# A streaming-encoder block on eight cores: pool branch over two blocks at once, group mixing folded into the output weights, conditioning by dot products

## The reference

```python
cc = silu(c)
mod = (cc @ w_ada + b_ada).reshape(b, 9, D)      # shift, scale, gate for three sub-layers
h = rms_norm(x, g_ffn1) * (1 + sc1) + sh1
x = x + 0.5 * gt1 * swiglu(h, w_ffn1_in, w_ffn1_out)
h = rms_norm(x, g_mix) * (1 + sc2) + sh2
z = h @ w_in                                      # q, k, v, u, gate A, gate B
ya = chunk_band_attention(q, k, v, ...) @ w_attn_out
mixed = trailing_mean(u, window of the group) - u
yb = (einsum(mixed, w_pool_group) * pool_scale) @ w_pool_out
x = x + gt2 * ((sigmoid(ga) * ya + sigmoid(gb) * yb) @ w_o)
h = rms_norm(x, g_ffn2) * (1 + sc3) + sh3
x = x + 0.5 * gt3 * swiglu(h, w_ffn2_in, w_ffn2_out)
```

## Time and profile before

| | us |
|---|---|
| median of 3 runs | 1546.69 (1546.11 to 1546.8) |
| the profiled execution, its own time | 1544.76 |
| its span on the slowest core (core 7) | 1543.2 |
| spans of the eight cores | 1537.7 to 1543.2 |
| TensorE busy | 1486.7 (96%) |
| VectorE busy | 815.5 (53%) |
| ScalarE busy | 451.3 (29%) |
| POOL busy | 119.4 (8%) |

### The profile page before, as it was taken

The page is one execution under the profiler, slowest core; times in us unless marked ns, Lnnn a source line. Parts: engine busy times, 40 slices in busy tenths (PEclk is TensorE's granted clock), DMA queues, the critical chain, the costliest instruction groups (busy, mean ns, idle before and its releaser), DMA issues.

```text
span 1543.2 us, 23259 instructions; the slowest of 8 cores (1537.7 to 1543.2 us)
## 1 busy us (share of the span) xinstructions
PE 1486.7 (96%) x8336; PEld 703.2 (46%) x8336; DVE 815.5 (53%) x1290; ACT 451.3 (29%) x630; POOL 119.4 (8%) x170
## 2 busy tenths in 40 slices
PE   2899999999999999999999999999999999999998
PEld 1344444444444444454564454444444444444443
DVE  2366344172272756678765568746453616162644
ACT  3470111101101036468855453523401010101010
POOL 1100100100001012200000000203000000000000
PEclk9999999999999999999999999999999999999999
DMA  9951433513515211430044363347132221211022
GB/s 204 243 102 28 76 69 55 99 25 69 96 28 102 48 41 38 123 60 15 1 93 86 56 130 63 69 82 116 28 55 53 44 42 16 47 28 28 1 110 109
DMA packets 24303, 107.13 MB, mean 69 GB/s; under 512 B 2816, under 2 KB 3072, under 8 KB 21760
## 3 DMA queue, kind: packets, MB, share of 16 engines
q0 software_dynamic: 21312, 75.67, 29.0%
q1 hardware_dynamic: 2880, 29.98, 5.6%
HBM read 168.71 MB, written 12.58 MB: 117 GB/s over the span
## 4 chain that ended last, share of the span: by engine, by line
PE 91%; DMA 3%; DVE 3%; issue 2%; ACT 1%; POOL 0%; DVEq 0%; ACTq 0%; POOLq 0%
PE ps L714 44%; PE ps L742 21%; PE ps L1081 7%; PE ps L887 4%; PE ps L1113 4%; PE ps L1094 3%; DMA arena<-w_ada 3%; PE ps L1027 2%; DVE arena L513 1%; PE ps L933 1%; PE ps L969 1%; PE ps L870 1%; DVE arena L519 1%; PE ps L563 1%; PE ps L609 1%
## 5 line engine op out<-in xcount | busy, mean ns | idle before, releaser
L714 PE MATMUL ps<-arena 128*128 128x512 bf16 x3152 | 694.4, 381 | 4.4 <-DVE arena L519 4.0
L507 ACT ACTIVATE arena<-ps 128x512 bf16<-128x512 f32 (+3 forms) x426 | 268.5, 652 | 946.3 <-PE ps L714 790.4
L714 PEld LDWEIGHTS ps<-arena 128*128 128x128 bf16 x3152 | 307.8, 98 | 376.3 <-issue 16.2
L519 DVE SCALAR_TENSOR_TENSOR arena<-ps,arena 128x512 f32<-128x512 f32 (+1 forms) x500 | 360.4, 748 | 73.6 <-ACT arena L507 22.6
L513 DVE TENSOR_TENSOR arena<-arena,ps 128x512 bf16<-128x512 bf16 x198 | 135.1, 687 | 486.8 <-PE ps L714 476.1
L742 PE MATMUL ps<-arena 128*128 128x512 bf16 x1584 | 345.0, 379 | 1.3 <-DVE arena L513 1.2
L742 PEld LDWEIGHTS ps<-arena 128*128 128x128 bf16 x1584 | 154.4, 98 | 188.3 <-issue 5.5
L513 DVE TENSOR_TENSOR arena<-arena 128x1024 f32<-128x1024 f32 (+8 forms) x228 | 173.6, 780 | 33.8 <-ACT arena L507 27.6
L1081 PE MATMUL ps<-arena 128*128 128x512 bf16 x512 | 116.3, 379 | 1.4 <-ACT arena L507 1.0
L507 ACT ACTIVATE arena<-arena 128x512 f32<-128x512 f32 (+2 forms) x86 | 89.3, 1053 | 35.2 <-DVE arena L519 20.8
L1081 PEld LDWEIGHTS ps<-arena 128*128 128x128 bf16 x512 | 49.1, 98 | 59.8 <-issue 2.4
(11 more groups left out here) (65 smaller groups left out, 516.6 us busy)
## 6 DMA issues: line engine op xcount, KB each, us to landing
arena<-w_ada POOLq DMA_DIRECT2D x36, 512.0 KB, 8.8
arena<-w_gate POOLq DMA_DIRECT2D x24, 512.0 KB, 8.5
arena<-w1i POOLq DMA_DIRECT2D x22, 512.0 KB, 6.5
arena<-w3i POOLq DMA_DIRECT2D x22, 512.0 KB, 5.3
arena<-x SPq DMA_DIRECT2D x5, 2048.0 KB, 15.5
outT<-arena SPq DMA_DIRECT2D x8, 1024.0 KB, 3.9
arena<-w1o POOLq DMA_DIRECT2D x10, 512.0 KB, 6.8
arena<-w_kqvu POOLq DMA_DIRECT2D x10, 512.0 KB, 7.6
```

Source lines behind the costliest of these rows:

```text
L507: return e.activation(out=o, in_=i, func=func, scale=scale)
L519: return e.scalar_tensor_tensor(out=out, in0=in0() if callable(in0) else in0, scalar=scalar, in1=in1() if callable(in1) else in1, op0=op0, ...
L714: ins = e.matmul(pst(t), lhsT=w[:, kt, :], rhs=hk(b, kt), start=(kt == 0), stop=(kt == 7))
```

## The change

- The pool branch treats both blocks of a pass as one row of 16 + 1024 columns. The history is copied once per group, the additions run over up to 1040 columns, the subtraction over 1024.
- Group mixing and pool scale go into the pool output weights: `fold()`, ahead of the third group of the first FFN, scales the (now transposed) group weights on VectorE, multiplies them with w_pool_out in 8 matmuls of 512 columns, evicts on ScalarE and stores the bf16 result in the first block's part of the output tensor, from which `gates` reads it through SP's queue. The mixing matmul, its scaling and POOL's load of the group weights go. The last store of that block waits for the reads.
- Columns 24 to 71 of the conditioning (groups 12 to 35) are computed on VectorE: w_ada's transpose comes in 48 fp32 tiles of 128x1024 through SP's queue into two buffers, and one `scalar_tensor_tensor` each multiplies it with the silu of c on every partition and sums along the row. They run behind three of every four units from the 23rd on.
- `norm_apply` gives six of eight tiles to ScalarE in the second and third sub-layer, three of eight in the first as before.
- The matmuls of `outp` also wait for the gate's row; the last block is stored in pieces of 4, 2, 1 and 1 tiles where it was 4 and 4.
- Some planned costs and all due times in `RAMPS` are other numbers.

```diff
-RAMPS = {"v0a": (6.86, 12.16), "k0a": (10.15, 11.87), "k0b": (10.76, 11.77), "v0b": (12.6, 12.7),
...
+RAMPS = {"v0a": (15.71, 38.08), "k0a": (10.87, 12.53), "k0b": (11.92, 12.65), "v0b": (18.64, 26.23),
...
+    def ada_dot(j, deps=()):
+        wt = ADS[j % 2]
+        S.op("sp", lambda e: e.dma_start(out=wt, in_=adat_d[j - 24]), writes=[wt], dma="d_ads%d" % (j % 2), nbytes=1 << 19,
+             deps=deps)
+        S.op("dve", lambda e: e.scalar_tensor_tensor(out=wt, in0=wt, scalar=1.0, in1=CCB, op0=ALU.mult, op1=ALU.mult,
+                                                     accum_out=MOD[:, j:j + 1]),
+             reads=[wt, CCB], writes=[wt, MOD[:, j:j + 1]], cost=1.22)
...
-                if kt in (1, 4, 7):
+                if kt in ((1, 4, 7) if sub == 0 else (0, 1, 3, 4, 6, 7)):
...
+    def fold():
+        pgf = view(wslot("f"), F32, (4, 128))
+        S.op("sp", lambda e: e.dma_start(out=pgf, in_=wpg_d.rearrange("p (g n) -> p g n", g=4)), writes=[pgf], dma="d_wpg",
+             nbytes=1 << 18)
+        for g in range(4):
+            ts(WPG[:, g, :], pgf[:, g, :], CST[:, 106 + g:107 + g], ALU.mult, [pgf, CST], [WPG], 0.2)
+        wps = [load("f", po_d[q])[0] for q in range(2)]
+        outs = [view(wslot("f"), BF16, (2048,)) for _ in range(2)]
+        for g in range(4):
+            for hf in range(2):
...
+                S.op("pe", lambda e, t=t, g=g, src=src: e.matmul(pst(t), lhsT=WPG[:, g, :], rhs=src, start=True, stop=True),
+                     reads=[WPG, wps[g // 2]], writes=[t], cost=mmc(1, 512))
...
+        for hf in range(2):
+            ov = outs[hf].bitcast(F32)
+            FOLD.append(S.op("sp", lambda e, ov=ov, hf=hf: e.dma_start(
+                out=outT[0].rearrange("p a b -> p (a b)")[:, 1024 * hf:1024 * (hf + 1)], in_=ov),
+                reads=[outs[hf]], dma="d_fold%d" % hf, nbytes=1 << 19))
...
-            if ada_next[0] < 36 and n > 20 and n % 3 == 0:
-                c = ada_next[0]
-                ada_load(c, [uops[max(0, n - 7)]])
-                t = Tile()
-                ada_mm(c, t, c)
-                ada_out(t, c, 1)
+            if ada_next[0] < 72 and n > 22 and n % 4 != 0:
+                j = ada_next[0]
...
+                ada_dot(j, [uops[max(0, n - 4)]])
...
-                            for n in range(0, 8, 4):
...
+                            for n, w in ((0, 4), (4, 2), (6, 1), (7, 1)) if b == blocks[-1] else ((0, 4), (4, 4)):
...
+                if first and g == 2:
+                    fold()
...
-                mx = MIXED[:, gq, mb * TB:(mb + 1) * TB]
-                stt(mx, src[:, 16:528], 1.0 / (2 << gq), ub[:, 16:528], ALU.mult, ALU.subtract, [src, ub], [mx], 0.75)
...
-                S.op("pe", lambda e, ty=ty, gq=gq, mx=mx: e.matmul(pst(ty), lhsT=WPG[:, gq, :], rhs=mx, start=True, stop=True),
-                     reads=[WPG, mx], writes=[ty], cost=mmc(1, 512))
-                ts(mx, lambda ty=ty: pst(ty), CST[:, 106 + gq:107 + gq], ALU.mult, [ty, CST], [mx], 0.7)
...
+                tt(dst[:, lo:1040], src[:, lo:1040], src[:, lo - sh:1040 - sh], ALU.add, [src], [dst], 1.28)
...
+            mx = MIXED[:, gq, :]
+            stt(mx, src[:, 16:1040], 1.0 / (2 << gq), ub[:, 16:1040], ALU.mult, ALU.subtract, [src, ub], [mx], 1.45)
...
-            wap = load("m", gate_d[3 * c + 2])[0]
...
+            S.op("pool", lambda e, c=c, wap=wap: e.dma_start(out=wap[:, 0:1024], in_=ao_d[c]), writes=[wap[:, 0:1024]],
+                 dma="d_w%d" % o_ap, nbytes=1 << 19)
+            wpf = view(o_ap + 2048, F32, (512,))
+            USES.append(S.op("sp", lambda e, c=c, wpf=wpf: e.dma_start(
+                out=wpf, in_=outT[0].rearrange("p a b -> p (a b)")[:, 512 * c:512 * (c + 1)]), writes=[wap[:, 1024:2048]],
+                dma="d_wf%d" % o_ap, nbytes=1 << 18, deps=[FOLD[c // 2]]))
```

More of the change, by code:

```diff
@@ L383, in build_nc @@
     cst_d = din("cst", [128, NCST])
-    ada_d = din("w_ada", [36, 128, 2048])
+    ada_d = din("w_ada", [12, 128, 2048])
+    adat_d = din("w_adat", [48, 128, 1024])
+    crow_d = din("crow", [128, 1024])
     w1i = din("w1i", [22, 128, 2048])
@@ L389, in build_nc @@
     kqvu_d = din("w_kqvu", [8, 128, 2048])
-    gate_d = din("w_gate", [12, 128, 2048])
+    gate_d = din("w_gate", [8, 128, 2048])
+    ao_d = din("w_ao", [4, 128, 1024])
+    po_d = din("w_po", [2, 128, 2048])
     wo_d = din("w_o", [4, 128, 2048])
@@ L585, in der @@
                  reads=[src], writes=[dst])
+    ADS = [view(o_expb + 4096 * i, F32, (1024,)) for i in range(2)]
+    CCB = view(o_kq, BF16, (1024,))
+    def ada_dot(j, deps=()):
[5 more added lines that the diff above has]
+             reads=[wt, CCB], writes=[wt, MOD[:, j:j + 1]], cost=1.22)
     rk_pos = [0]
@@ L744, in mm @@
                     return ins
-                S.op("pe", mm, reads=[w for w in wos] + [ACTB[:, jl, b, :] for jl in range(nk)], writes=[t],
+                S.op("pe", mm, reads=[w for w in wos] + [ACTB[:, jl, b, :] for jl in range(nk)] + [DER[:, 3 * sub + 2, :]], writes=[t],
                      cost=mmc(nk, 512))
@@ L832, in build_nc @@
     ffn(w1i, w1o, 0, [0, 1, 2, 3, 4], True)
-    S.op("pool", lambda e: e.dma_start(out=WPG, in_=wpg_d.rearrange("p (g n) -> p g n", g=4)), writes=[WPG], dma="d_wpg",
-         nbytes=1 << 18, deps=[S.ops[-1]])
     S.op("pool", lambda e: e.dma_start(out=IDENT, in_=ident_d), writes=[IDENT], dma="d_idn", nbytes=1 << 16,
@@ L1017, in u_stage @@
                 ts(UH[:, gq, :], lambda th=th: pst(th, 0, 16), CST[:, 110:111], ALU.mult, [th, CST], [UH[:, gq, :]], 0.17)
+            S.op("dve", lambda e, gq=gq: e.tensor_copy(out=ub[:, 0:16], in_=UH[:, gq, :]), reads=[UH[:, gq, :]],
+                 writes=[ub[:, 0:16]], cost=0.17)
             for mb in range(2):
@@ new lines, in u_stage @@
+            src = ub
+            for st in range(gq + 1):
+                sh = 1 << st
+                dst = TTS[st % 2]
+                lo = 2 * sh - 1
+                tt(dst[:, lo:1040], src[:, lo:1040], src[:, lo - sh:1040 - sh], ALU.add, [src], [dst], 1.28)
+                src = dst
+            mx = MIXED[:, gq, :]
+            stt(mx, src[:, 16:1040], 1.0 / (2 << gq), ub[:, 16:1040], ALU.mult, ALU.subtract, [src, ub], [mx], 1.45)
+            if pas == 0:
+                t16 = TTS[(gq + 1) % 2]
+                tt(t16[:, 0:16], src[:, 16:32], CST[:, 112 + 16 * gq:128 + 16 * gq], ALU.mult, [src, CST],
+                   [t16[:, 0:16]], 0.17)
+                tt(MIXED[:, gq, 0:16], t16[:, 0:16], ub[:, 16:32], ALU.subtract, [t16[:, 0:16], ub],
+                   [MIXED[:, gq, 0:16]], 0.17)
@@ L1238, in _prep @@
         gates.append(_cols(w_in, 3072 + 256 * cc, 256))
-        gates.append(np.concatenate([_cols(w_ao, 256 * cc, 256), _cols(w_po, 256 * cc, 256)], 1))
+        gates.append(_cols(w_ao, 256 * cc, 256))
     shared = {
-        "w_ada": np.stack([_cols(w_ada, 256 * cc, 256) for cc in range(36)]),
+        "w_ada": np.stack([_cols(w_ada, 256 * cc, 256) for cc in range(12)]),
+        "w_adat": w_ada.T[3072:].reshape(48, 128, 1024),
         "w1i": ffn_in(f("w_ffn1_in")[0]),
@@ L1246, in _prep @@
         "w_kqvu": np.stack([_cols(w_in, c0, 256) for c0 in (512, 768, 0, 256, 1024, 1280, 1536, 1792)]),
-        "w_gate": np.stack(gates),
+        "w_gate": np.stack([g for cc in range(4) for g in gates[3 * cc:3 * cc + 2]]),
+        "w_ao": np.stack(gates[2::3]),
+        "w_po": np.ascontiguousarray(w_po.reshape(2, 2, 128, 1024).transpose(0, 2, 1, 3).reshape(2, 128, 2048)),
         "w_o": np.stack([_cols(f("w_o")[0], 256 * cc, 256) for cc in range(4)]),
@@ L1250, in _prep @@
         "ident": np.eye(128, dtype=np.float32),
-        "w_pg": np.ascontiguousarray(f("w_pool_group")[0].transpose(1, 0, 2).reshape(128, 512)),
+        "w_pg": np.ascontiguousarray(pgT),
     }
```

69 lines of the change are left out of this document (35 added, 34 removed), and 8 rows, old and new, of the table RAMPS.

## The result

The changed kernel took 1555.87 us (median of 4 runs, 1555.28 to 1558.68), the kernel before 1546.4 beside it: ratio 1.0069, 95% interval 1.0054 to 1.0084. It is slower by 9.5 us where 17.0 less were forecast. (In the experiments, executions in which one die had a lower granted clock are left out, and every time is the median of the others.)

A forecast was written before the change was run, and what follows sets the result against it. TensorE, busy 96% of the span, was taken as the bound. Terms 9.4 - 0.5 + 4.9 - 2.0 + 2.0 + 2.0 + 1.2 = 17.0 us off 1544.76 gave 1527.8, with the median's 1.9 1529.7; range 1519 to 1541.5.

The forecast's parts named there:

- Conditioning off TensorE, gain 9.4: First FFN: 24 w_ada groups of 0.38 us leave TensorE, 9.1 us, plus 0.3 us of one load wait.
- The dots' loads, 0.5 charged: First FFN: 0.5 us (0 to 5) charged for dots delaying VectorE; with loads landing in 4 us, none late.
- a mean threshold of 7.4 us: First FFN, late-dots rival: landings above 7.4 us hold VectorE and TensorE; at 8.3 us landing, 1551 us; chance 0.06.
- POOL's queue loses 24 loads, its weights can only come earlier: POOL's load queue: without 24 conditioning loads, the remaining weight loads could not become later; no cost charged.
- covered by the 24 slot uses that went: Weight ring of nine slots: the fold's one use of five slots costs nothing, as 24 conditioning uses left.
- The mixer's order, bounds of 9.6 either way: Mixer: replanned order could gain 9.6 us (no wait left) or lose 9.6 (twice the waits).
- The rival that the new order loses: Mixer: shuffled order doubles the waits, taking 2.0 + 9.6 us from the sum, 1541.3 us; chance 0.17.
- Branch on VectorE, gain 2.0: Mixer: pool branch over 1024 columns relieves VectorE by about 22 us, of which 2.0 us reach the end.
- the 1.4 and 2.0 of the forecast: Mixer idle time of TensorE: 1.4 us from the removed group matmuls' waits, 2.0 us from the branch's relief.
- The fold, 2.9 net: Group matmuls leaving the mixer gain 4.9 us; fold's matmuls and wait in the first FFN lose 2.0.
- Scale-shift, gain 2.0: Block norms before the mixer: VectorE freed 1.5 us earlier, gaining 1.5 plus 0.5 us; range 0 to 4.6.
- Last stores, gain 1.2: End of the kernel: smaller last pieces land earlier, gaining 1.2 us, with 0 to 1.7 or 2.9 considered.

The follow-up runs named there:

- late6: Changed kernel with the planner counting 6 us more for the landing of each dot's load: 1546.95 us, ratio 1.0027 to the kernel before.
- dots6: Kernel before plus only the conditioning dots, their loads counted 6 us later, old due times, large weight ring started 6 slots later: 1534.12 us, ratio 0.9944.
- retuned: Whole change, dots' loads counted 6 us later, ring started at slot 3, fold one group earlier, due times searched anew: 1529.47 us, ratio 0.9909.
- dots6n: dots6 with the planner's old count of a load's landing, 2 us instead of 8 for the dots: 1536.42 us, ratio 0.9956.
- dots0: dots6 with the large weight ring started at slot 0 instead of 6: 1544.15 us, ratio 1.0007.
- turn0: Whole change with dots' loads counted 6 us later and the due times of before, ring at slot 0: 1561.06 us, ratio 1.0117.
- turn3: turn0 with the large weight ring started 3 slots later: 1542.3 and 1542.6 us in two executions, no interval.
- ring5: Changed kernel with the large weight ring started 5 slots later: 1559.25 us, ratio 1.0111 to the kernel before.
- early_v: late6 with every engine's order and PSUM banks frozen, ring started 6 slots later, mixer's first loads ordered V, V, K, K, Q, Q: 1545.66 us, ratio 1.0017.
- both: Changed kernel with the edits of ring5 and late6 together: 1548.73 us, ratio 1.0035 to the kernel before.
- pool4: Kernel before plus only two-block pool branch, fold, last stores and changed planned costs; old due times, ring started 4 slots later: 1555.74 us, ratio 1.0078.
- fold4: pool4 with the pool branch one block at a time again, the mixing still folded: 1545.59 us, ratio 1.002.
- d6norm: dots6 plus the new scale-shift split, six of eight on ScalarE outside the first FFN: 1535.04 us, ratio 0.9942.
- d6stores: dots6 plus the last block's stores in pieces of 4, 2, 1 and 1: 1533.53 us, ratio 0.9937.

## Why the prediction was wrong

The sum by stage, us of the profiled executions: first the terms of the prediction applied to the kernel before (first FFN 648.8 - 9.4 + 0.5 + 2.0 - 1.5; mixer 430.4 - 4.9 - 2.0 - 0.5), then what was measured. The stages end with the start of the last matmul of the first FFN, of the first of the second, and of the last; the tail ends the span.

| | forecast | before | after | late6 | dots6 | retuned |
|---|---|---|---|---|---|---|
| first FFN ends | 640.4 | 648.8 | 652.5 | 643.8 | 638.6 | 639.5 |
| mixer | 423.0 | 430.4 | 438.5 | 438.3 | 429.6 | 426.5 |
| second FFN | 458.5 | 458.5 | 458.2 | 458.2 | 458.5 | 457.3 |
| tail | 4.3 | 5.5 | 4.7 | 4.8 | 5.8 | 4.7 |

The forecast missed by 12.1 us in the first FFN and by 15.5 in the mixer. Two steps of the prediction failed: that no dot's data would be late, and that the mixer's new order could lose no more than its waits of before, with the turn of the slots put at nothing.

**Conditioning off TensorE, gain 9.4: right.** dots6 shows it: its first FFN ends 10.2 us earlier, and it is 0.56% or 8.6 us faster. The dot at 1.22 + 0.08 us was right.

**The dots' loads, 0.5 charged: the first step that failed.** The landing taken, 4 us, was near the median of 4.7. But the step weighed only a mean against a mean threshold of 7.4 us. TensorE stops for a single late load, for all of VectorE's wait beyond 4.0 us: 15.9 us to landing beside the fold's stores and the weights. It said that SP's queue was otherwise idle, and did not ask what shares the DMA engines; the fold's own loads and stores were counted as hidden, and they fell into the same place. Cost, from late6: 0.42% by the ratios, 6.5 us; 8.7 us in the table's first FFN. dots6n puts some 2 us on the planner's low count without the fold. That the landings of 16 us come with the fold is shown by the runs with and without it; that they make the rest of the cost is read from the trace, as the fold was never moved alone. What a late landing costs depends on where the plan has put its dot: retuned has one of 16.0 us too, and its TensorE idles 0.6 us from 172 to 545.

**"POOL's queue loses 24 loads, its weights can only come earlier", and the fold's five slots "covered by the 24 slot uses that went": wrong, the root of the second step that failed.** I counted slots and not their turn. The V weight was asked for at 654.49 where it had been 641.64. With the due times of before, the turn alone is worth 10 us to the dots (dots0, dots6) and some 19 to the whole change (turn0, turn3). And an earlier weight is not a gain in itself: dots0 and ring5 have their V weights earlier and are slower. early_v shows why: the wait is handed on, and what counts is the order that is planned around the weights. With its own due times the changed kernel gained nothing from another turn (ring5, both), so the turn is not shown to be the whole cause of its loss.

**The mixer's order, bounds of 9.6 either way: too narrow, the second step that failed.** Of the 15.5 us, 11.6 are idle time of TensorE: 19.3 us in the mixer, where it had been 11.6 and 3.9 less were forecast. The hole at the start makes most of it, 11.7 us up to 670 where it had been 1.6. The other 3.9 are matmuls: 16 fewer, and yet TensorE was busy for 419.2 us where it had been 418.8, with the granted clock at 0.98 in the mean of the mixer instead of 1.00. The rival that the new order loses was the right kind of case, priced at 11.6 us from the sum and looked for among attention's steps; the mixer alone lost 15.5. Doubling the waits of a good order does not bound a bad one: with the same parts and due times, the turn alone moved the mixer from 451.1 us (turn0) to 434.7 (turn3), and new due times, with the fold one group earlier, to 426.5 (retuned).

**Branch on VectorE, gain 2.0: not shown.** The idle time from 670 to 1090 fell by 3.4 us, the 1.4 and 2.0 of the forecast, but by chance: 1.07 us of the 11.0 that I took for the mixer's are a wait of the second FFN, at 1083.86, and that stage begins only at 1091.0 in the changed kernel. (The 4.0 us of the earlier trace rows that I called the longest wait are the sum of two, this one and the 2.96 at 629.) From 670 to the mixer's own end the fall is 2.4, and pool4 shows that relief of VectorE need not bring any. **The fold, 2.9 net: not shown alone.** fold4, with the due times of before, is 0.2% slower than before. retuned's mixer is 3.1 us shorter than that of dots6 and its first FFN 0.9 longer, so 2.2, with the branch and the due times in it. **Scale-shift, gain 2.0: not seen**, neither at 545 to 645 (3.5 idle us, 3.2 before) nor in d6norm. **Last stores, gain 1.2:** 0.8 in the table, the tail 4.7 instead of 5.5; but dots6, with the old stores, has 5.8 and d6stores, with the new, 5.5.

retuned gains 0.91% or 14 us on the kernel before, 15.2 in the profiled executions, of the 17.0 that the terms add up to. So most of what the changed kernel lost was not in its parts, but in their place and order. (That its 1529.47 is next to the forecast of 1529.7 is chance: the kernel before took 1543.6 beside it, not 1546.69.) What stays open is how the 15.5 us in the mixer divide between turn and due times at the changed kernel's own due times, since each change of either rewrites the order.

## What to carry to other kernels

Taking loads out of a ring of buffers, or adding some, changes which buffer every later load gets: list the slots around the next change of stage, and restore the turn with an offset before judging the edit. That was worth 10 us to the dots; it was not enough for branch and fold (pool4). A greedy planner's order is as large a term as the work itself (here 25 us in a 430 us mixer), so test a part with the order kept, or search the order anew for both. For an engine that runs in order, judge loads by the latest single landing against the place that the plan gives its user, with all that is under way at that moment, and not by their median or the sum of the waits.

## What was not expected of the hardware

A 512 KB load on SP's queue landed in 4.7 us in the median and in 15.9 beside two 512 KB stores and four 512 KB weight loads. VectorE could wait 71.0 us for data in the first FFN while TensorE lost 2.8, as no single wait was over 5.1 and 4.0 of each were hidden. A subtraction of two fp32 streams over 1024 columns took 1.223 us, as long as the dot with its one bf16 stream, 1.224. The Trainium skill (Vector Engine (DVE) Microarchitecture Reference, section 7) says that such an instruction with two sources other than bf16 halves its rate, which these rows don't show. And the hole at the mixer's start is paid twice: after TensorE had stood waiting there, the granted clock was 0.76 in the mean of 645 to 670, and 0.83 to 0.91 from 640 to 680 in the experiments with such a wait, where dots6 and retuned had 1.00.
